# Joins filled with early panels, one DVE operation per hgrn level, softmax division on ACT, filter loads on SP

## The reference

```
sc = einsum(q, k_all) * dh ** -0.5;  p = softmax(sc);  o = einsum(p, v_all)      # layer 0 of block 2
```

## Time and profile before

| | |
|---|---|
| median of 3 runs | 2466.38 us (2466.13 to 2469.29) |
| profiled execution | 2468.29 us |
| its span | 2466.2 us |
| PE busy | 2340.2 us, 95% of the span |
| DVE busy | 1808.7 us, 73% |
| ACT busy | 1386.3 us, 56% |
| POOL busy | 40.6 us, 2% |
| mean granted TensorE clock | 0.98 |
| loaded | 531.8 MB, 496 panels |

### The profile page before, as it was taken

How to read it: one execution, slowest core, us unless ns; L and a number is a source line. 1 busy time by engine, 2 the same in 40 slices (tenths; PEclk the granted TensorE clock), 3 DMA queues, 4 the chain that set the end, 5 groups by cost and what they waited for, 6 DMA issues and landing times. The chain is left out here.

```text
span 2466.2 us, 34542 instructions
## 1 busy us (share of the span) xinstructions
PE 2340.2 (95%) x13639; PEld 2015.2 (82%) x13639; DVE 1808.7 (73%) x1730; ACT 1386.3 (56%) x1381; POOL 40.6 (2%) x42
## 2 busy tenths in 40 slices
PE   7998999999798899999999999999989999799988
PEld 7898899998798788888888888888866875668977
DVE  6664556557755589888988898889876757856684
ACT  6463544546364477777777777777753322534363
POOL 0100000000100000000000000000001000000100
PEclk9999999999999899999999999999999999999999
DMA  6234467664233299989999999999970220025300
GB/s 253 89 137 151 172 241 249 244 234 143 86 137 137 104 364 365 367 341 368 366 367 341 369 361 370 342 366 359 374 293 35 86 103 1 1 73 120 99 1 18
DMA packets 81797, 531.80 MB, mean 216 GB/s; under 512 B 16935, under 2 KB 17224, under 8 KB 17480
## 3 DMA queue, kind: packets, MB, share of 16 engines
q1 hardware_dynamic: 80704, 525.22, 57.7%
q10 hardware_dynamic: 968, 4.78, 0.6%
HBM read 528.91 MB, written 1.05 MB: 215 GB/s over the span
## 5 line engine op out<-in xcount | busy, mean ns | idle before, releaser
L2327 DVE TENSOR_TENSOR ring_low<-ring,M_high 128x2048 fp32r<-128x2048 f32 x336 | 760.8, 2290 | 105.2 <-ACT M_high L1319 97.9
L1319 ACT ACTIVATE M_high<-ring 128x2048 fp32r<-128x2048 f32 x336 | 632.3, 1910 | 2.6 <-DMA ring<-panels 1.9
L464 PE MATMUL ps<-M_high,xe_parts 128*128 128x512 f32 x1344 | 449.0, 397 | 2.0 <-DVE ring_low L2327 2.0
L464 PEld LDWEIGHTS ps<-M_high,xe_parts 128*128 128x128 f32 x1344 | 252.4, 188 | 54.0 <-issue 2.4
L464 PE MATMUL ps<-ring_low,xe_parts 128*128 128x512 f32 x672 | 261.9, 390 | 0.0
L2197 DVE TENSOR_TENSOR W_low<-ring,W_high 128x2048 fp32r<-128x2048 f32 x66 | 150.0, 2291 | 101.7 <-ACT W_high L1319 101.7
L464 PE MATMUL ps<-h_parts,ring_low 128*128 128x256 f32 x704 | 204.4, 290 | 0.0
L464 PE MATMUL ps<-h_parts,B_high 128*128 128x256 f32 x1024 | 193.8, 291 | 5.6 <-DVE h_parts L1959 5.1
L464 PE MATMUL ps<-M_high,hid_high 128*128 128x512 f32 x448 | 175.9, 393 | 2.2 <-DVE hid_low L2333 2.2
L1319 ACT ACTIVATE arena<-ps 128x256 f32<-128x256 f32 (+3 forms) x210 | 101.9, 485 | 131.4 <-PE ps L464 119.3
L1319 ACT ACTIVATE W_high<-ring 128x2048 fp32r<-128x2048 f32 x66 | 124.6, 1908 | 89.2 <-PE ps L464 89.2
(11 more groups left out here) (300 smaller groups left out, 4887.6 us busy)
## 6 DMA issues: line engine op xcount, KB each, us to landing
ring<-panels SPq DMA_DIRECT2D x496, 1024.0 KB, 4.8
arena<-rpb SPq DMA_DIRECT2D x32, 64.0 KB, 8.2
cst<-consts SPq DMA_DIRECT2D x1, 1632.0 KB, 12.2
xT<-x SPq DMA_DIRECT2D x1, 1024.0 KB, 4.9
cT<-ctx ACTq DMA_DIRECT2D x1, 1024.0 KB, 8.2
arena<-dft ACTq DMA_DIRECT2D x1, 1024.0 KB, 11.5
y<-xT ACTq DMA_DIRECT2D x1, 1024.0 KB, 3.9
proj<-w ACTq DMA_DIRECT2D x1, 512.0 KB, 8.3
```

What stands on the lines that cost most here:

```text
L464: return nc.tensor.matmul(o, w, m, start=start, stop=stop, skip_group_check=skip)
L1319: return nc.scalar.activation(o, i, fn, **kw)
L2327: V.tensor_tensor(wide_low(q, 0, PW), ring[:, (q % RING) * PW:(q % RING + 1) * PW], moe_high(q, 0, PW).bitcast(F32), ALU.subtract).then_in ...
```

## The change

1. `DENSE` starts with cond 0 and cond 1, ahead of gate 0, and ends with cond 22 and 23. ACT copies the first three of these panels among the squares of the norm and the fourth ahead of the h copies; DVE splits the first three inside `mix_out`. The last pair is multiplied behind the mean squares of layer 1's norm, its turn behind layer 1's first panel, and `conditioned()` moves behind the splits of panels 1 and 2.
2. In both layers' `project1`, ACT copies panel 1 ahead of the norm's h copies. In layer 1 the homes of panels 1 and 2 are exchanged.
3. hgrn levels: POOL's half is gone. DVE writes both halves of X in one operation of 1024 elements; k and q swap their places in the arena.
4. MoE start: ACT copies panel 2 ahead of `hN_high`; DVE splits panel 1 ahead of the second token half.
5. MoE end: the last expert's rows are scaled, split and scattered in two halves. The eight loads are issued by SP, after the loads of panels BLOCK1+1 and BLOCK1+4 (SP's hardware loop ends earlier for it).
6. Block 2, layer 0: ACT's query copies carry the scale -0.125, so the reduction takes a minimum and its result is the exponential's bias (L2681 gone); the low part becomes a scalar_tensor_tensor; the division moves to ACT, between the exponential of unit i and the turned copy of unit i-2.
7. Block 2, layer 1: panels in the order 0, 1, 3, 2, 4, ...; copies, splits and pair copies of turns 2 and 3 stand inside the context's chunks.
8. The mask is added to the bias table in four operations of 1024 elements, in DVE's turns 9 to 12 of `project2`, ahead of `announce("qk_done")`.

```diff
-DENSE = [("gate", 0), ("up", 0)]
+DENSE = [("cond", 0), ("cond", 1), ("gate", 0), ("up", 0)]
 ...
+    _pair = 2 <= _f < ADA
 ...
-DENSE += [("down", FSTEP - 1)]
+DENSE += [("down", FSTEP - 1), ("cond", 2 * ADA - 2), ("cond", 2 * ADA - 1)]
+PANEL_ORDER = (tuple(range(IN2)), (0, 1, 3, 2) + tuple(range(4, IN2)))
 ... SP
-            looped = last_mixer // RING
+            looped = BLOCK1 // RING
 ...
+                if p == BLOCK1 + 1:
+                    ... w1, position, w2, w3, context
+                elif p == BLOCK1 + 4:
+                    ... decay, skip, dft
 ... PE, project1 and the loop over the layers
+                    if i == 0 and behind_first:
+                        behind_first()
 ...
+                    last_pair()
+                    project1(layer, last_turn)
 ... PE, MoE end
-                scatter(E - 1, range(4))
+                scatter(E - 1, (0, 1))
+                pe.wait_ge(sem("rows_split"), E + 1)
+                scatter(E - 1, (2, 3))
 ... ACT, project1
+                proj_part(layer, p0, 1)
                 for k in range(KD):
                     act.wait_ge(sem("h_ready"), nth(act, "h_ready"))
                     f(h_parts[:, k, S:512], h3[:, k, 0:S], ACT.Copy).then_inc(sem("h_parts_high"), 1)
-                proj_part(p0, 1)
-                proj_part(p0, 2)
+                if layer:
+                    act.wait_ge(DONE, p0)
+                    conditioning_rows(ADA - 1)
+                proj_part(layer, p0, 2)
 ... ACT, norm of the feed-forward part
-                    if j == 3 and layer == 0:
+                    if layer == 0 and j == 2:
                         high_part(panel[0], 0, 0)
+                        high_part(panel[0] + 1, -1, 0)
+                    elif layer == 0 and j == 3:
+                        high_part(panel[0] + 2, -2, 0)
                     square_pair(j)
                 norm_root(S, MEAN_BANK[1])
                 if layer == 0:
+                    high_part(panel[0] + 3, 0, 0)
                     dense_layer(panel[0])
 ...
+                    moe_panel_high(panel[0] + 2)
                     act.wait_ge(sem("h_turned"), nth(act, "h_turned"))
                     f(hN_high, bank(0, 4), ACT.Copy).then_inc(sem("h_tokens_copied"), 1)
 ... ACT, modulated_high and attend
+                    if behind and (k, s) in ((1, 1), (5, 1)):
+                        behind(k // 4)
 ...
+                def divided(j):
+                    act.wait_ge(sem("probs_sum_inverted"), j + 1)
+                    pr = probs(layer, j)[:, 0:us[j]["keys"]]
+                    f(pr, pr, ACT.Copy, scale=stat[:, 12 + j % 4:13 + j % 4]).then_inc(sem("probs_ready"), 1)
 ...
-                            f(pr[:, 0:u["keys"]], bank(b + i % 2)[:, 0:u["keys"]], ACT.Exp, bias=nm, scale=0.125,
+                            f(pr[:, 0:u["keys"]], bank(b + i % 2)[:, 0:u["keys"]], ACT.Exp, bias=nm, scale=-1.0,
                               accum_out=acc).then_inc(sem("probs_scaled_exp"), 1)
+                            if i:
+                                divided(i - 1)
 ... DVE, level
-                    w = lambda a: a.rearrange("p (n two b) -> p n two b", two=2, b=B)[:, :, 1, :]
-                    signal(V.tensor_tensor(w(X), w(q), w(E[lv % 2]), ALU.mult), "level_q_ready")
+                    w = lambda a: a.rearrange("p (n two b) -> p n two b", two=2, b=B)
+                    base = arena[:, 0:1024]
+                    qk = bass.AP(base.tensor, base.offset, [base.ap[0], [2 * B, 512 // B], [1024 + B, 2], [1, B]])
+                    signal(V.tensor_tensor(w(X), qk, w(E[lv % 2]), ALU.mult), "level_qk_ready")
 ... DVE, project2
+                            if (k, s) in ((3, 1), (7, 1)):
+                                narrow_part(p0, 2 + k // 4)
 ...
+                    if layer == 1 and 9 <= p < 13:
+                        if p == 9:
+                            dve.wait_ge(sem("position_bias_landed"), 16 * 32)
+                        m = K(K_NBR, S).unsqueeze(1).to_broadcast([P, 4, S])
+                        b = arena[:, (p - 9) * 1024:(p - 8) * 1024].rearrange("p (a n) -> p a n", a=4)
+                        step(V.tensor_tensor(b, b, m, ALU.add))
 ... DVE, attend
-                            step(V.tensor_reduce(mx, bank(score_bank + i % 2)[:, 0:u["keys"]], AX.X, ALU.max))
-                            signal(V.tensor_scalar(nm, mx, -0.125, None, ALU.mult), "max_ready")
+                            signal(V.tensor_reduce(nm, bank(score_bank + i % 2)[:, 0:u["keys"]], AX.X, ALU.min),
+                                   "max_ready")
 ...
+                        if layer == 0:
+                            signal(V.reciprocal(rs, total), "probs_sum_inverted")
+                        else:
+                            step(V.reciprocal(rs, total))
+                            signal(V.tensor_scalar(pr, pr, rs, None, ALU.mult), "probs_ready")
```

More of the change, by code:

```diff
@@ L1103, in mean_square @@
                         .then_inc(sem("qk_mean_square"), 1)
-                for p in range(IN2):
+                for turn, p in enumerate(PANEL_ORDER[layer]):
                     q = at[0]
@@ L1151, in project2 @@
                     for i in range(len(chunks)):
-                        if swaps[i] == p and chunks[i][3]:
+                        if swaps[i] == turn and chunks[i][3]:
                             swap(i)
@@ L1619, in _ @@
                 if layer:
-                    proj_part(panel[0], 0)
+                    proj_part(layer, panel[0], 0)
                 for j in range(4):
@@ L1729, in narrow_part, with pair_copy @@
                     .then_inc(sem("wide_panel_high"), 1)
+            def pair_copy(layer, p0, turn):
+                if turn + 2 < IN2:
+                    narrow_part(p0, turn + 2)
+                p = PANEL_ORDER[layer][turn]
+                wide = layer == 0 or p in (2, 5, 6, 7, 8)
+                o = proj[:, 2 * p * 512:(2 * p + 2) * 512]
+                i = bank(2 * (turn % 2), 2)
+                if not wide:
+                    o = o.rearrange("q (a n) -> q a n", a=2)[:, :, 0:S]
+                    i = i.rearrange("q (a n) -> q a n", a=2)[:, :, 0:S]
+                if layer == 0 and p == 2:
+                    act.wait_ge(sem("filter_spectrum_ready"), 2)
+                act.wait_ge(DONE, p0 + turn + 1)
+                f(o, i, ACT.Silu if p >= 9 else ACT.Copy).then_inc(sem("pair_copied"), 1)
             def project2(layer):
@@ L1852, in attend @@
                     else:
+                        if layer == 0 and i == n:
+                            divided(n - 1)
                         turned_copy(i - 2)
@@ L2189, in mix_out @@
                 for j in range(OUTP):
+                    if layer == 0 and j >= 2:
+                        for i in ((0,), (1, 2))[j - 2]:
+                            low_part(p0 + 2 * OUTP + i, i + 1)
                     multiplied(1)
```

263 lines of the change are left out of this document (126 added, 137 removed).

## The result

The changed kernel takes 2436.8 us (median of 4 runs, 2431.9 to 2446.9) against 2466.3 for the kernel before; the ratio is 0.9883, with a 95% interval of 0.9861 to 0.9906. That is 29.5 us or 1.2%, while single executions of the changed kernel lie 15 us apart. Four further executions had a median of 2437.0 and a ratio of 0.9876 (0.9861 to 0.9891). The forecast was 2438.1, in a range of 2430 to 2449.

A forecast was written before the change was run, and what follows sets the result against it. PE was taken as the bound, busy 2340.2 of 2466.2 us, leaving short holes to fill. Gains hole by hole summed to 28.3 us, taking the profiled 2468.3 to 2440.0, so the median forecast was 2438.1, range 2430 to 2449.

The forecast's parts named there:

- G: Layer 0's attention, block 2: multiplication removed, division moved to ACT, PE next at about 1.72 us per unit; gain 4.3 us.
- D: MoE start: panel 1's split and panel 2's copy moved earlier remove PE's wait of 1.97 us; gain 1.8 us.
- E: MoE end: loads issued by SP and rows done in halves remove ACT's 3.92 and PE's 4.30 us; gain 4.4 us.
- the early copy at the start: Kernel's start: panel 1 copied ahead of the norm's h copies, as at the second join; gain 0.25 us.
- level 0: First hgrn level, q and k alternating element by element: merged operation taken at 2.05 us, no gain; 0.8 per layer at 1.22.
- H1: Layer 1's join, block 2: panel 3 ahead of panel 2 shrinks PE's 4.37 us hole to 0.9; gain 4.9 to 5.0.
- A: First join: two cond panels fill PE's 3.75 us hole before gate 0; gain 3.9 us.
- B: Second join: two cond panels fill PE's 4.14 us hole before layer 1, panel 1 comes 1.8 earlier; gain 5.7 us.
- the clock doesn't come back: Rival, 13%: cond panels at 1.2 GHz in both joins, no clock gain at block 2's layer-1 join; 2443 us.
- C: hgrn levels: one merged DVE operation saves 0.46 us in each of four cycles, 1.84 per layer; gain 3.7 us.
- ACT becomes attention's bound: Rival, 12%: with the division, ACT's busy 6.3 us per four units plus semaphore gaps reaches 7.3, attention gains 0; 2442.4 us.
- H2: Bias in layer 1, block 2: four pieces delay panel 12's split and qk_done, so PE's scores wait for POOL; loss 0.75 us.

The follow-up runs named there:

- levels alone: Kernel before with one part: DVE writes both halves of X in one operation, POOL's half gone; span 5.8 us shorter.
- loads alone: Kernel before with only the eight filter and context loads moved to SP, rows kept whole; last hidden split to taps 30.0 us, before 32.1.
- the run at full clock: Changed kernel with three bias pieces in DVE's turn 7, the fourth behind panel 12's split, qk_done in turn 9; panel 11 to first exponential 16.35 us against 20.29.

## Why the prediction was right, and where not

The sum was 28.3 us; the profiled execution lost 32.1, the medians 29.5. The total is nearer than its parts deserve. G failed in its main step, by the prediction's own sign: "if ACT's division leaves the attention at 7.29 per four units", and it did. What was too large (D by 0.8, E by 0.6, G by 1.05, the bias by 0.5, the early copy at the start by all of its 0.25) was made up by what was left out or too small (level 0: 1.1, H1: 0.7, A and B: 0.5), and by clock that the sum did not have (2.0 in D, 1.6 in out2). That they cancel is luck.

**The joins (A, B, H1)** were right as mechanisms and in size: 4.3, 5.8 and 5.7 against 3.9, 5.7 and 5.0. Each is PE's hole of before filled with work that had its inputs. In A the hole closed to 1.00 and the wait for up 0's low part stayed (1.08 for 1.23), as I had it. In H1 0.30 was left of the hole where I had 0.9. I took nothing for the clock in A and B, and it came back: the windows of the two joins went from 0.72 and 0.58 to 1.00. The rival "the clock doesn't come back" is refuted: the kernel before and the two runs on it (levels alone, loads alone) all have a low stretch right behind each of the three holes, and none of the eleven traces of the changed kernel and its variants has one there. In A its 1.4 us bought only 0.4, since panel gate 0 is paced by the h chain, as the prediction said of panel 0. The 0.25 for the early copy at the kernel's start did not come. Up to the levels the changed kernel is 0.2 us behind (PE's last row ahead of the first X starts at 55.56, before at 55.37), and its first panel had waited 2.41 us for h where before's waited 0.93. Whether the copy, which now stands ahead of h, caused that was not tested.

**C, levels.** The step "0.46 in each of four cycles per layer" holds: 1.96 and 2.00 measured, 1.84 forecast, cycles of 10.89 against my 10.9. The term mis-sized is level 0, taken at 2.05 with no gain; it took 1.48, and the 0.55 on layer 1's way to the first X is that, as is the 0.36 at the start of layer 0, less the 0.2 lost there. The Trainium skill, Vector Engine (DVE) Microarchitecture Reference, section 5.2, says that runs of two words keep the full rate and an element-wise hop doesn't. The trace agrees for level 1 and above (1.23) and in sign for level 0; its figure of 1.73 ns per column, an estimated 1.85 us, was too high for this pattern; and the two halves, which at level 0 step over every second word, were no slower there than elsewhere (0.69), against its rule. Here the measurement decides. The Trainium skill, GPSIMD Engine Reference, section 1, says that POOL shares its SBUF interfaces with VectorE and contends with DVE instructions of two SBUF inputs. The trace agrees: 0.69 us alone, 1.36 to 2.05 beside POOL. That is the row I lacked and had to bound.

**D, MoE start.** PE's wait of 1.97 went, 0.46 of it came back at the hidden split and 0.5 at an issue: about 1.0 by waits, where I had 1.8. The other 2.0 of the 2.98 was clock, which I had not counted. Neither holds still: in the second traced execution the gain was 1.66, with 1.10 at the hidden split for 1.61 and one more low stretch.

**E, MoE end.** Right as a mechanism, 3.8 for 4.4. The term "with SP issuing them, both go" was too large: the single part gave 2.0, because ACT's squares stand behind DVE's adds anyway; the halves, with what else is ahead of the taps, gave 1.8 where I had 1.05.

**G, layer 0's attention: the step failed.** I wrote "No engine was full ... So PE is next, with 1.6 to 1.7 per unit against 1.82". The steady part stayed at 7.30 us per four units (7.29 before); nothing of "24 x 0.1" came. The waits in the changed kernel:

```profile
DVE stat L2739 <- PE ps L483: 11.9, 16, 1.2
PEld ps L1282 <- ACT arena L1353: 7.6, 12, 0.9
PE ps L1282 <- ACT arena L1353: 4.2, 8, 0.6
```

PE's transposes wait for ACT's division, DVE's maximum waits for PE. I had counted the move as one step exchanged for another 0.07 to 0.13 longer. One unit in the run with the division on DVE, DVE and then ACT:

```profile
2095.79 0.35 DVE L2756 TENSOR_SCALAR arena<-arena,stat 128x256 f32<-128x256 f32 x1
...
2095.59 0.69 ACT L1353 ACTIVATE arena<-ps,stat 128x512 f32<-128x512 f32 x1 [1.03 <-DVE stat L2735]
```

and in the changed kernel, on ACT:

```profile
2092.64 0.69 ACT L1353 ACTIVATE arena<-ps,stat 128x512 f32<-128x512 f32 x1 [0.93 <-DVE stat L2739]
2093.22 0.19 ACT L1353 ACTIVATION_READ_ACCUMULATOR arena<-ps,stat 128x1 f32 x1
2093.32 0.50 ACT L1353 ACTIVATE arena<-arena,stat 128x256 f32<-128x256 f32 x1
```

On DVE the division of one unit ran beside ACT's exponential of the next and started 0.20 us after it; on ACT it stands behind the exponential and starts 0.68 or 0.45 us after it. It also takes 0.50 or 0.71 us there (256 or 512 keys) instead of 0.35 or 0.49, more than I had. Together the probabilities are ready 0.4 to 0.7 us later against the exponential. This took back what the removed multiplication gave: 7.29 before, 6.72 with the multiplication gone and the division on DVE, 7.30 with both edits. What saved the sum was the other term, the units in which DVE splits queries: 9.88 us became 7.82 for four, 2.1 where I had 1.0 for them, and another 1.2 before them. So my rival "ACT becomes attention's bound" had the steady gain right (0) and its reason wrong: with the same work on ACT three orders gave 7.05, 7.30 and 7.63.

**H2, the bias.** Right in sign and mechanism. PE's scores are released by POOL:

```profile
2315.81 3.04 PE L483 MATMUL ps<-proj 128*128 128x256 f32 x8 [3.56 <-POOL proj L1953]
```

and panel 12's split is 1.26 later for PE. The loss was 1.22 to the first exponential (0.75 forecast). The low clock at the scores had about 0.2 of it: 3.07 us from them to the exponential, 2.87 in the run at full clock, 2.84 in the changed kernel's second execution. With the pieces in the idle turn it is a gain of 2.7 over before (19.07 to 16.35), where I had 3.3.

**What I had not counted.** The clock outside the joins: 2.0 in D and 1.6 in out2 of layer 0, where before had a low stretch (2158 to 2164) and the changed kernel none, though nothing was changed there. That part is luck of the execution: the changed kernel's second execution has the stretch in out2 (2136 to 2140), and takes 58.5 us for it like before, not 56.9. What sets the places of these stretches stays open.

## What to carry to other kernels

Read an operation that moves to an idle engine by its place in that engine's order: what it ran beside, and what it will stand behind. In the steady part of attention here, taking DVE from 87% to 55% busy gained nothing, because the loop through all three engines became no shorter. And a signal should be announced as soon as what it promises is done, not behind unrelated work that was moved in front of it; that, with one piece of this work ahead of a split that PE waited for, cost 3.9 us here.

## What the runs showed of the hardware

- A DVE multiplication of 512 elements with both inputs in SBUF took 0.69 us alone and 1.36 to 2.05 beside a POOL multiplication that had started first, and ended 0.54 to 0.56 us after it in all 16 cases; POOL's copy of 256 elements took 0.40 alone and 1.0 to 2.5 beside DVE operations with two inputs, and a DVE addition of 1024 elements 1.22 alone and 1.4 beside POOL.
- One DVE operation whose source alternates between two places 4 KB apart at every element took 1.48 us for 1024 elements, and 1.23 where it alternates every second element or more rarely.
- The low stretches of PE's granted clock took 1.3 to 1.7 us of its busy time each, longer ones about 2 to 10. Between executions of one kernel their number differs, and with it the time: spans of the changed kernel of 2430.1, 2434.4, 2435.6 and 2445.1 us had mean clocks of 0.990, 0.987, 0.987 and 0.984.
- With matmuls of zeros in PE's holes at the router its clock fell as before (8.0 us lost for 7.7, in one execution each); with cond panels in the holes of the two norms it did not (windows at 1.00 for 0.72 and 0.58, in all eleven traces). What makes the difference was not tested.
